# Second mixer of a two-block kernel: score, transpose and value products regrouped on TensorE, two kinds of chunks read out two pieces later

## The chip, the cores and the metric

The kernel runs on one core of a Trainium2 chip, in one launch. The metric is the device time of one execution in microseconds (us), as the median of several runs.

## What is computed

The reference runs two blocks over 256 tokens of width 2048, in float32. The first block (a short gated convolution, a conformer convolution and pooling, then a gated MLP) is untouched by the change. The second begins with one large projection, whose columns feed four mLSTM heads and eight attention heads:

```python
xn = rmsnorm(x, norm_mix_pre[l])
proj = jnp.einsum('bsd,dc->bsc', xn, w_in[l])
mq, mk, mv, mo, mi, mf, aq, ak, av, g_m, g_a = split_cols(proj)
qk = jax.nn.silu(causal_depthwise_conv_2(jnp.concatenate([mq, mk], axis=-1), conv_w[l], conv_b[l]))
...
h = mlstm_chunkwise(mq_h, mk_h, mv_h, i_pre, f_pre)
h = h * lax.rsqrt(jnp.mean(h * h, axis=-1, keepdims=True) + NORM_EPS)
...
o_a = moba_attention(aq_h, ak_h, av_h)
```

At 256 tokens an mLSTM head is a causal product of decayed scores (q times k) with the values v, normalised, gated by o. An attention head is softmax(q k) times v over one block. After that come the merge with the gates g_m and g_a, the output projection and the second MLP.

## The kernel before, in words

The program is written engine by engine, with semaphores between them, and its order is written out by hand. Every weight matrix goes through the same conveyor, in **pieces** of 128 x 1024 numbers. SP's queue brings 1 MB blocks (two pieces) into `raw` (4 slots). ScalarE (ACT) copies a piece to the high half of `w_split` (L1138, `split`), VectorE (DVE) subtracts to make the low half (L1777, `split`), and TensorE (PE) multiplies: 8 tiles of three matmuls, 24 in all, per piece (L700 to L702; L792 to L794 where the tokens are the stationary operand). There are 4 slots of `w_split`, so ACT and DVE may make piece n only once PE has used piece n - 4. In this stage PE takes a piece in some 2.7 us, and DVE makes one in 1.2 us and has the rest of the time for everything else.

In the second mixer the projection goes in 28 **chunks** of four pieces (`CHUNKS2`). Chunk c is pieces 4c to 4c + 3. Per mLSTM head h they are q, k, v, o (chunks 4h to 4h + 3), then per pair of attention heads j aq, ak, av (chunks 16 + 3j and on). The merge's 24 pieces per turn follow, numbered from 112. Chunks 0 and 1 are an exception: they are opened together, q ending with piece 7 and k of the first head with piece 10 as DVE and ACT count them (`ends_2`: `{0: 7, 1: 10}`); every other chunk c ends with piece 4c + 3.

What is done at the end of a chunk stands in `chunk_end_2(c, o)`, called by ACT and DVE behind the split of the piece that comes o after the chunk's last one. DVE at o == 4 reads the chunk out of PSUM (`take_scaled`, `scale_tokens`, which count `pair_combined` up; PE waits on this before it starts the chunk after the next, which has the same PSUM bank). For q and k follow: ACT at o == 5 and DVE at o == 6 the short convolution into `q_m` and `k_m`, ACT at o == 7 a tanh, and DVE at o == 8 the last product (L1780, `q_m<-squares,q_m`), which counts `qk_ready` up. `o_m` and `a_v` are single buffers.

The products of the heads themselves are dropped in between pieces. `inner(piece_number)` calls on PE, ahead of a piece, `mlstm(h, stage)` where `piece_number - 16 * (h + 1)` is in `M_PE`, and `attention(j, stage)` where `piece_number - (64 + 12 * (j + 1))` is in `A_PE`:

- `mlstm` stage 0: the scores (L986), behind a wait `qk_ready` >= 2h + 2, that is, for both q_m and k_m of the head; stage 1: the values (L992 to L994); stage 2: four transposes of h_tok (L1001).
- `attention` stage 0: the scores of two heads (L1014, L1015); stage 1: transposes of the probabilities (L1022); stage 2: the values (L1032, L1034).

`M_ACT`, `M_DVE`, `A_ACT` and `A_DVE` hold the same kind of numbers for ACT's and DVE's share of a head. Below, "r" is a piece's number less 16(h + 1), and all these products are plain float32, where the pieces are float32r.

The two lines that set where PE stands before a head's products are these:

```python
r = piece_number - 16 * (h + 1)
if r in M_PE:
    mlstm(h, M_PE.index(r))
```

Of the kernel before, what the change touches and what calls it, by code (L numbers as in the profile page):

```python
# [93 lines left out]
def build(nc, xT, params, consts, positions, w_in, w_out, w_up, w_down,  # L94
# [22 lines left out]
    with ctx:  # L117
# [14 lines left out]
        def put(name, shape):  # L132

            at = cursor[0]
            cursor[0] += (4 * math.prod(shape[1:]) + 31) // 32 * 32
            return place(name, shape, at=at)
# [68 lines left out]
        o_m = put("o_m", [128, 2, T])  # L205
# [15 lines left out]
        a_v = put("a_v", [128, 2, T])  # L221
# [18 lines left out]
        def P(name, k=0, n=1):  # L240
            at = PARAM[name] + k
            return par[:, at:at + n] if isinstance(at, int) else par[:, bass.ds(at, n)]
# [9 lines left out]
        def bcast(row, tiles=2):  # L252

            return row.rearrange("p (a t) -> p a t", a=1).to_broadcast([128, tiles, T])


        def sem(name):
            return ctx.enter_context(nc.semaphore(name))
# [102 lines left out]
        m_gated = sem("m_gated")  # L361
# [9 lines left out]
        a_valued = sem("a_valued")  # L371
# [35 lines left out]

        M_PE, M_ACT, M_DVE = (4, 9, 14), (8, 13, 15, 19), (7, 9, 12, 14, 18, 20)  # L410
        A_PE = (2, 9, 12)
        A_ACT, A_DVE = ((6, 12, 15), (7, 12, 15)), ((5, 7, 16), (6, 9, 16))
        ROWS_STORED, SCALE_STORED = 18, 12

        BOUNDARY_SPLITS = {N_PREF1: {3: (5,), 5: (6,), 6: (7,)}, N_PRE2: {3: (5,), 5: (6, 7)},
# [18 lines left out]
        def at_least(eng, s, value):  # L434

            if not isinstance(value, int) or value > 0:
                eng.wait_ge(s, value)
# [66 lines left out]
        def pair2(c):  # L504
            return qW2 + c - 1

        def last_of(first, c):

            return first(NARROW * c + 3 + {0: 4, 1: 1}.get(c, 0))
# [61 lines left out]
        def tiles_of(bank):  # L571
            return ps[:, bank, :].rearrange("p (a t) -> p a t", a=2)
# [124 lines left out]
        def _(pe):  # L697
# [340 lines left out]
            def inner(piece_number):  # L1038
# [9 lines left out]
                for j in range(4):  # L1048
                    r = piece_number - (64 + 12 * (j + 1))
                    if r in A_PE:  # L1050
                        attention(j, A_PE.index(r))

# [69 lines left out]
        def _(act):  # L1122
# [17 lines left out]
            def combined(q):  # L1140
                act.wait_ge(pair_combined, q.value(PAIR_CREDIT + 1))
# [304 lines left out]
            for g, n in enumerate(GROUPS1):  # L1446
# [13 lines left out]
                last = g == len(GROUPS1) - 1  # L1460
# [33 lines left out]
            def chunk_end_2(c, o):  # L1494

                kind, h = CHUNKS2[c]
                q = Step(pair2(c))
                if o == 5 and kind in ("q", "k"):
                    is_k = int(kind == "k")
                    out = (q_m, k_m)[is_k]  # L1500
                    if c > 1:
                        combined(q)
                    else:
                        act.wait_ge(opened, 2 + c + 1)
                    at_least(act, m_scored, h)
                    source = k_in if c == 1 else qk_in
                    for t in range(2):
                        k = 8 * is_k + 2 * h + t
                        nc.scalar.activation(out[:, t, :], source[:, t, 3:3 + T], ACT.Identity,
                                             scale=P("conv_w_2", 48 + k), bias=P("conv_b_2", k)  # L1510
                                             ).then_inc(qk_started, 1)
                elif o == 7 and kind in ("q", "k"):
                    is_k = int(kind == "k")
                    act.wait_ge(qk_convolved, 2 * h + is_k + 1)
                    nc.scalar.activation(squares[:, is_k, :, :], (q_m, k_m)[is_k][:, :, :], ACT.Tanh, scale=0.5
                                         ).then_inc(qk_tanh, 1)
                elif o == 5 and kind == "o":
                    combined(q)
                    nc.scalar.activation(o_m[:, :, :], o_m[:, :, :], ACT.Tanh, scale=0.5).then_inc(o_ready, 1)

# [228 lines left out]
        def _(dve):  # L1749
# [26 lines left out]
            def tt(out, a, b, op):  # L1776
                return nc.vector.tensor_tensor(out, a, b, op)  # L1777

            def stt(out, a, scalar, b, op0, op1):
                return nc.vector.scalar_tensor_tensor(out=out, in0=a, scalar=scalar, in1=b, op0=op0, op1=op1)  # L1780
# [9 lines left out]
            def summed(last):  # L1790

                dve.wait_ge(piece_used, last.value(USED_CREDIT + 1))

            def take_scaled(last, bank, out):

                summed(last)
                tt(out, tiles_of(bank), bcast(pre_scale[:, :]), ALU.mult).then_inc(pair_combined, 1)

            def scale_tokens(last, bank, out):

                summed(last)
                dve.wait_ge(pre_col_loaded, 16)
                for s in range(2):
                    ins = nc.vector.tensor_scalar(out[:, s, 0:T], ps[:, bank + s, 0:T], pre_col[:, s:s + 1], None,
                                                  ALU.mult)
                ins.then_inc(pair_combined, 1)
# [6 lines left out]
            def combined(q):  # L1813
                dve.wait_ge(pair_combined, q.value(PAIR_CREDIT + 1))
# [502 lines left out]
            def chunk_end_2(c, o):  # L2317
                kind, h = CHUNKS2[c]
                q, last, bank = Step(pair2(c)), Step(last_of(piece2, c)), 2 * ((c + 1) % 2)
                is_k = int(kind in ("k", "ak"))  # L2320
                if o == 4:
                    if kind in ("q", "k"):
                        if c > 1:
                            at_least(dve, qk_convolved, 2 * h + is_k)
                            take_scaled(last, bank, qk_in[:, :, 3:3 + T])
                    elif kind == "v":
                        at_least(dve, m_valued, h)
                        scale_tokens(last, bank, v_tok)
                    elif kind == "av":
                        at_least(dve, a_valued, 2 * h)  # L2330
                        scale_tokens(last, bank, a_v)
                    elif kind == "o":
                        at_least(dve, m_gated, h)
                        take_scaled(last, bank, o_m[:, :, :])
                    else:
                        at_least(dve, a_scored, 2 * h)
                        take_scaled(last, bank, {"aq": a_q, "ak": a_k}[kind][:, :, :])
                elif o == 6 and kind in ("q", "k"):
                    out = (q_m, k_m)[is_k]
                    for k in (2, 1, 0):  # L2340
                        for t in range(2):
                            if k == 2:
                                dve.wait_ge(qk_started, 4 * h + 2 * is_k + t + 1)
                            else:
                                dve.wait_ge(vector_step, steps.all(but=1))
                            ins = stt(out[:, t, :], (k_in if c == 1 else qk_in)[:, t, k:k + T], P("conv_w_2", 16 * k + 8 * is_k + 2 * h + t),
                                      out[:, t, :], ALU.mult, ALU.add)
                            if (k, t) == (0, 1):
                                ins.then_inc(qk_convolved, 1)
                            else:  # L2350
                                ins.then_inc(vector_step, steps.one())
                elif o == 8 and kind in ("q", "k"):
                    out = (q_m, k_m)[is_k]
                    dve.wait_ge(qk_tanh, 2 * h + is_k + 1)
                    stt(out[:, :, :], squares[:, is_k, :, :], 1.0, out[:, :, :], ALU.add, ALU.mult
                        ).then_inc(qk_ready, 1)
                elif o == 5 and kind in ("aq", "ak"):
                    a = (a_q, a_k)[is_k]
                    combined(q)
                    dve.wait_ge(table_step, 3)  # L2360
                    at_least(dve, rope_ready, 2 * h + is_k)
                    for lo_, hi_ in ((0, 64), (64, 0)):
                        for t in range(2):
                            tt(scaled[lo_:lo_ + 64, 0, t, :], a[hi_:hi_ + 64, t, :],
                               sin[hi_:hi_ + 64, :], ALU.mult).then_inc(vector_step, steps.one())
                    dve.wait_ge(vector_step, steps.all())
                    tt(a[:, :, :], a[:, :, :], bcast(cos[:, :]), ALU.mult).then_inc(vector_step, steps.one())
                    dve.wait_ge(vector_step, steps.all())
                    tt(a[:, :, :], a[:, :, :], scaled[:, 0, :, :], ALU.add).then_inc(rope_ready, 1)
# [278 lines left out]
```

## Time and profile before

| what | value |
|---|---|
| median of 3 runs | 2422.86 us (2422.09 to 2423.03) |
| the profiled execution's own time | 2421.82 us |
| its span, first to last instruction | 2420.0 us |
| PE busy | 2409.3 us (100%) |
| PE weight loads busy | 2395.4 us (99%) |
| DVE busy | 1631.7 us (67%) |
| ACT busy | 1186.5 us (49%) |
| SP's queue | 456.34 MB, 58.1% of the 16 DMA engines' span |
| HBM read | 455.15 MB, 189 GB/s over the span |
| mean granted TensorE clock | 0.999 |

The span is 1.8 us under the execution's own time, and that is 1.0 us under the median. A busy PE says only that matmuls follow one another closely: they are pipelined, each lasts 276 ns in the records, and in the steady parts one starts every 113 ns. So what counts is the distance of two starts. In a timeline row the first number is the start, the second the duration, and "xN" says how many instructions are merged; a float32 matmul counts as two passes there, a transpose as one. A window row gives the stretch, its length, the busy time and number of instructions (x) of PE, weight loads (PEld), DVE, ACT and POOL (only PE and PEld where it is asked for one line), then the granted clock as a share of 2.4 GHz, the DMA engines' busy share and GB/s.

### The profile page before, as it was taken

What the parts mean: (1) busy time and instruction counts of PE and PEld (TensorE: products, weight loads), DVE (VectorE), ACT (ScalarE), POOL (GpSimd) and SP (SyncE); (2) the same over time, 40 slices, a digit from 0 to 9 for tenths busy, and PEclk for the clock granted to TensorE, in tenths of its full rate; (3) what the DMA queues carried; (4) which work ended last, traced back from release to release, by engine and by line L of the source; (5) the groups of instructions that cost most, each with busy time, mean ns of one, the idle gap of its engine ahead of it and who ended that gap; (6) DMA issues with size and microseconds to landing.
All of it is one profiled execution on the core that took longest, in us unless ns stands there. A gap on an engine that the chain in (4) does not pass through costs nothing. (4 is left out here: it accounts for less than half of the span.)

```text
span 2420.0 us, 49137 instructions
## 1 busy us (share of the span) xinstructions
PE 2409.3 (100%) x20938; PEld 2395.4 (99%) x20938; DVE 1631.7 (67%) x2088; ACT 1186.5 (49%) x1434; POOL 58.9 (2%) x57
## 2 busy tenths in 40 slices
PE   9999999999999999999999999999999999999999
PEld 9999999999999999999999999999999999999998
DVE  8998687765776567697677655554865554555554
ACT  6445655534554455666544444445543443443444
POOL 0300100000000000100000000001000000000001
PEclk9999999999999999999999999999999999999999
DMA  8565555565555555565555566655555655655652
GB/s 286 185 192 192 175 197 196 182 208 192 191 191 194 194 195 192 167 206 175 178 179 171 185 187 196 194 193 192 171 195 194 193 198 194 196 192 191 192 193 104
DMA packets 308084, 459.64 MB, mean 190 GB/s; under 512 B 14789, under 2 KB 156370, under 8 KB 307922
## 3 DMA queue, kind: packets, MB, share of 16 engines
q1 hardware_dynamic: 304112, 456.34, 58.1%
q8 instruction: 126, 2.06, 0.3%
q10 hardware_dynamic: 3810, 0.94, 0.2%
q14 instruction: 36, 0.29, 0.0%
HBM read 455.15 MB, written 2.11 MB: 189 GB/s over the span
## 5 line engine op out<-in xcount | busy, mean ns | idle before, releaser
L1777 DVE TENSOR_TENSOR w_split<-raw,w_split 128x1024 fp32r<-128x1024 f32 (+1 forms) x856 | 1047.2, 1225 | 747.3 <-ACT w_split L1138 744.8
L1138 ACT ACTIVATE w_split<-raw 128x1024 fp32r<-128x1024 f32 x853 | 900.6, 1060 | 1064.6 <-PE ps L702 1020.3
L700 PE MATMUL ps<-h_split,w_split 128*128 128x256 f32 x3904 | 1081.6, 277 | 0.3 <-DVE w_split L1777 0.3
L701 PE MATMUL ps<-h_split,w_split 128*128 128x256 f32 x3904 | 1078.4, 276 | 0.0
L702 PE MATMUL ps<-h_split,w_split 128*128 128x256 f32 x3904 | 1078.3, 276 | 0.0
L700 PEld LDWEIGHTS ps<-h_split,w_split 128*128 128x128 f32 x3904 | 732.9, 188 | 0.9 <-DVE w_split L1777 0.5
L701 PEld LDWEIGHTS ps<-h_split,w_split 128*128 128x128 f32 x3904 | 732.9, 188 | 0.3
L702 PEld LDWEIGHTS ps<-h_split,w_split 128*128 128x128 f32 x3904 | 732.8, 188 | 0.0
L700 PE MATMUL ps<-act_split,w_split 128*128 128x256 f32 x2240 | 619.3, 276 | 0.0
L701 PE MATMUL ps<-act_split,w_split 128*128 128x256 f32 x2240 | 618.3, 276 | 0.0
L702 PE MATMUL ps<-act_split,w_split 128*128 128x256 f32 x2240 | 618.3, 276 | 0.0
L701 PEld LDWEIGHTS ps<-act_split,w_split 128*128 128x128 f32 x2240 | 420.4, 188 | 0.1
L700 PEld LDWEIGHTS ps<-act_split,w_split 128*128 128x128 f32 x2240 | 420.4, 188 | 0.1
L702 PEld LDWEIGHTS ps<-act_split,w_split 128*128 128x128 f32 x2240 | 420.4, 188 | 0.0
L1780 DVE SCALAR_TENSOR_TENSOR conv_b<-glu,par,conv_b 128x256 f32<-128x256 f32 x180 | 80.4, 501 | 0.0
L792 PE MATMUL ps<-w_split,h_split 128*128 128x256 f32 x256 | 72.2, 282 | 0.0
L793 PE MATMUL ps<-w_split,h_split 128*128 128x256 f32 x256 | 71.0, 277 | 0.0
L794 PE MATMUL ps<-w_split,h_split 128*128 128x256 f32 x256 | 71.0, 277 | 0.0
L700 PE MATMUL ps<-merged,w_split 128*128 128x256 f32 x256 | 70.9, 277 | 0.0
L702 PE MATMUL ps<-merged,w_split 128*128 128x256 f32 x256 | 70.7, 276 | 0.0
L701 PE MATMUL ps<-merged,w_split 128*128 128x256 f32 x256 | 70.7, 276 | 0.0
L1725 POOL TENSOR_TENSOR square_sum<-squares 128x512 f32<-128x512 f32 x4 | 6.6, 1647 | 2081.9 <-ACT squares L1151 2081.9
(290 smaller groups left out, 1613.3 us busy)
## 6 DMA issues: line engine op xcount, KB each, us to landing
raw<-w_up SPq DMA_DIRECT2D x152, 1024.0 KB, 5.1
raw<-w_in SPq DMA_DIRECT2D x114, 1024.0 KB, 5.3
raw<-w_down SPq DMA_DIRECT2D x108, 1024.0 KB, 5.0
raw<-w_out SPq DMA_DIRECT2D x32, 1024.0 KB, 5.0
raw<-w_in SPq DMA_DIRECT2D x16, 512.0 KB, 5.2
raw<-w_branch_m SPq DMA_DIRECT2D x8, 1024.0 KB, 5.3
raw<-w_branch_a SPq DMA_DIRECT2D x8, 1024.0 KB, 5.3
outT<-x SPq DMA_DIRECT2D x7, 256.0 KB, 2.3
```

The source lines that it names most:

```text
L700: nc.tensor.matmul(out, hi[:, cols], rhs[:, k, 0:T], start=start, stop=False)
L701: nc.tensor.matmul(out, hi[:, cols], rhs[:, k, T:2 * T], start=False, stop=False)
L702: return nc.tensor.matmul(out, lo[:, cols], rhs[:, k, 0:T], start=False, stop=stop)
L792: nc.tensor.matmul(out, high, pair[:, 0, cols], start=k == 0, stop=False)
L793: nc.tensor.matmul(out, high, pair[:, 1, cols], start=False, stop=False)
L794: last = nc.tensor.matmul(out, rest, pair[:, 0, cols], start=False, stop=k == 15)
L1138: nc.scalar.activation(split_home(n)[0], raw[:, slot, half:half + 1024], ACT.Copy).then_inc(hi_ready, 1)
L1725: nc.gpsimd.tensor_tensor(square_sum[:, :, :], square_sum[:, :, :] if q > 1 else squares[:, 0, :, :], squares[:, q % 2, :, :], ALU.add).th ...
L1777: return nc.vector.tensor_tensor(out, a, b, op)
L1780: return nc.vector.scalar_tensor_tensor(out=out, in0=a, scalar=scalar, in1=b, op0=op0, op1=op1)
```

## The change

Two tables of numbers and two readouts are different:

- `M_PE` goes from (4, 9, 14) to (0, 9, 16). Head h's scores now stand ahead of piece 16(h + 1), four pieces earlier. Its transposes stand ahead of piece 16(h + 2), two pieces later, in front of the next head's scores. Its share on DVE and ACT behind the transposes is one piece later (18 to 19, 20 to 21; 19 to 20).
- `A_PE` goes from (2, 9, 12) to (2, 9, 14). A pair's values now stand in front of the next pair's scores, and what DVE and ACT do with them is two pieces later (16 to 18; 15 to 17).
- The o chunks and the av chunks are read out at o == 6, not at o == 4, and ACT's tanh of o comes at o == 7, not at o == 5.

```diff
-        M_PE, M_ACT, M_DVE = (4, 9, 14), (8, 13, 15, 19), (7, 9, 12, 14, 18, 20)
-        A_PE = (2, 9, 12)
-        A_ACT, A_DVE = ((6, 12, 15), (7, 12, 15)), ((5, 7, 16), (6, 9, 16))
+        M_PE, M_ACT, M_DVE = (0, 9, 16), (8, 13, 15, 20), (7, 9, 12, 14, 19, 21)
+        A_PE = (2, 9, 14)
+        A_ACT, A_DVE = ((6, 12, 17), (7, 12, 17)), ((5, 7, 18), (6, 9, 18))
...
-                elif o == 5 and kind == "o":
+                elif o == 7 and kind == "o":
                     combined(q)
                     nc.scalar.activation(o_m[:, :, :], o_m[:, :, :], ACT.Tanh, scale=0.5).then_inc(o_ready, 1)
...
-                    elif kind == "av":
-                        at_least(dve, a_valued, 2 * h)
-                        scale_tokens(last, bank, a_v)
-                    elif kind == "o":
-                        at_least(dve, m_gated, h)
-                        take_scaled(last, bank, o_m[:, :, :])
-                    else:
+                    elif kind in ("aq", "ak"):
                         at_least(dve, a_scored, 2 * h)
                         take_scaled(last, bank, {"aq": a_q, "ak": a_k}[kind][:, :, :])
+                elif o == 6 and kind == "av":
+                    at_least(dve, a_valued, 2 * h)
+                    scale_tokens(last, bank, a_v)
+                elif o == 6 and kind == "o":
+                    at_least(dve, m_gated, h)
+                    take_scaled(last, bank, o_m[:, :, :])
```

**TensorE, the first head's scores.** `w_split0` to `w_split3` are the four slots; the rows before are the end of piece 15 (slot 1), the start of piece 16 (slot 2), and, four pieces on, the end of piece 19 (slot 1 again) with the scores behind it.

```order
6472 L702 MATMUL ps<-h_split_55,w_split1_51 128x256
6473 L700 MATMUL ps<-h_split_55,w_split2_52 128x256 [waits lo_ready,pair_combined]
...
6568 L702 MATMUL ps<-h_split_55,w_split1_51 128x256
6569 L986 MATMUL ps<-q_m_88,k_m_89 128x256 [waits qk_ready,pair_combined]
6570 L986 MATMUL ps<-q_m_88,k_m_89 128x256
6571 L986 MATMUL ps<-q_m_88,k_m_89 128x128 x2
```

The same place in the changed kernel:

```order
6472 L702 MATMUL ps<-h_split_55,w_split1_51 128x256
6473 L986 MATMUL ps<-q_m_88,k_m_89 128x256 [waits qk_ready,pair_combined]
6474 L986 MATMUL ps<-q_m_88,k_m_89 128x256
6475 L986 MATMUL ps<-q_m_88,k_m_89 128x128 x2
6476 L700 MATMUL ps<-h_split_55,w_split2_52 128x256 [waits lo_ready]
```

The first head's scores, with their wait for `qk_ready`, have moved from behind piece 19 to right behind piece 15, with no transposes in front of them, since there is no head before.

**VectorE, the same stretch.** These rows run from the split of piece 16 to that of piece 21, in the kernel before; the changed one has the same rows as far as number 870.

```order
859 L1777 TENSOR_TENSOR w_split2_52<-raw_49,w_split2_52 128x1024 [waits hi_ready]
860 L1780 SCALAR_TENSOR_TENSOR k_m_89<-k_in_106,par_57,k_m_89 128x256 [waits qk_started] x2
861 L1780 SCALAR_TENSOR_TENSOR k_m_89<-k_in_106,par_57,k_m_89 128x256 [waits vector_step] x4
862 L1777 TENSOR_TENSOR w_split3_53<-raw_49,w_split3_53 128x1024 [waits hi_ready]
...
868 L1777 TENSOR_TENSOR w_split0_50<-raw_49,w_split0_50 128x1024 [waits hi_ready]
869 L1780 SCALAR_TENSOR_TENSOR k_m_89<-squares_61,k_m_89 128x512 [waits qk_tanh]
870 L1777 TENSOR_TENSOR w_split1_51<-raw_49,w_split1_51 128x1024 [waits hi_ready]
871 L1777 TENSOR_TENSOR o_m_90<-ps,pre_scale_66 128x512 [waits piece_used]
872 L1777 TENSOR_TENSOR w_split2_52<-raw_49,w_split2_52 128x1024 [waits hi_ready]
873 L1777 TENSOR_TENSOR w_split3_53<-raw_49,w_split3_53 128x1024 [waits hi_ready]
```

The last product of the first head's k_m (869) stands behind the split of piece 18 (868), before and after the change; what moved is the readout of o_m, from 871 to behind 873.

**TensorE, transposes and the next head's scores** in the changed kernel, ahead of piece 32, the first pair of this kind; the transposes stood alone ahead of piece 30, the scores alone ahead of piece 36.

```order
6863 L1001 MATMUL ps<-con_58,h_tok_94 128x128 [waits h_tok_ready,pair_combined]
6864 L1001 MATMUL ps<-con_58,h_tok_94 128x128 x3
6865 L986 MATMUL ps<-q_m_88,k_m_89 128x256 [waits qk_ready]
6866 L986 MATMUL ps<-q_m_88,k_m_89 128x256
6867 L986 MATMUL ps<-q_m_88,k_m_89 128x128 x2
6868 L700 MATMUL ps<-h_split_55,w_split2_52 128x256 [waits lo_ready]
```

Of the 23 places between pieces at which the heads' products interrupted the projection 18 are left: three pairs of heads' transposes and scores and three of values and scores now share a place, and the last mLSTM head's transposes, which shared one with the first attention pair's scores (ahead of piece 78), stand alone ahead of piece 80.

## Rows read from the trace of the kernel before

**Rows 1.** The page, busy time of the engines.

```profile
PE 2409.3 (100%) x20938; PEld 2395.4 (99%) x20938; DVE 1631.7 (67%) x2088; ACT 1186.5 (49%) x1434; POOL 58.9 (2%) x57
```

**Rows 2.** Window over the second mixer: busy time of PE, PEld, DVE, ACT, POOL.

```profile
1041.00:1401.00 360.00, 360.00 (x3079) 357.73 (x3078) 265.22 (x429) 189.54 (x260) 0.00 (x0) 1.00 0.59 181
```

**Rows 3.** Waits of PE in the whole span: in total, times, longest.

```profile
PE ps L700 <- DVE w_split L1777: 0.3, 1, 0.3
```

**Rows 4.** Timeline of PE: transposes alone, scores alone, both together.

```profile
1105.62 0.28 PE L702 MATMUL ps<-h_split,w_split 128*128 128x256 f32 x1
...
1106.29 0.28 PE L701 MATMUL ps<-h_split,w_split 128*128 128x256 f32 x1
...
1283.64 0.28 PE L702 MATMUL ps<-h_split,w_split 128*128 128x256 f32 x1
...
1285.18 0.28 PE L701 MATMUL ps<-h_split,w_split 128*128 128x256 f32 x1
...
1246.91 0.28 PE L702 MATMUL ps<-h_split,w_split 128*128 128x256 f32 x1
1247.03 0.60 PE L1001 MATMUL ps<-con,h_tok 128*128 128x128 f32 x4
...
1248.89 0.28 PE L701 MATMUL ps<-h_split,w_split 128*128 128x256 f32 x1
```

**Rows 5.** Timeline of PE, and line L700 in a window: pieces 12 to 19.

```profile
1053.24 0.28 PE L794 MATMUL ps<-w_split,h_split 128*128 128x256 f32 x1
...
1053.36:1064.44 11.08, 8.90 (x32) 5.99 (x33) 1.00 0.62 189
...
1064.44 0.28 PE L700 MATMUL ps<-h_split,w_split 128*128 128x256 f32 x1
...
1069.98 0.38 PE L700 MATMUL ps<-h_split,w_split 128*128 128x256 f32 x1
...
1075.55 1.47 PE L986 MATMUL ps<-q_m,k_m 128*128 128x256 f32 x8
```

**Rows 6.** Timeline of DVE, first head: k_m's convolution to its last product.

```profile
1062.55 2.46 DVE L1780 SCALAR_TENSOR_TENSOR k_m<-k_in,par,k_m 128x256 f32<-128x256 f32 x6
1064.93 1.22 DVE L1777 TENSOR_TENSOR w_split<-raw,w_split 128x1024 fp32r<-128x1024 f32 x1
...
1068.72 1.21 DVE L1777 TENSOR_TENSOR w_split<-raw,w_split 128x1024 fp32r<-128x1024 f32 x1
1069.86 0.67 DVE L1780 SCALAR_TENSOR_TENSOR k_m<-squares,k_m 128x512 f32<-128x512 f32 x1
```

**Rows 7.** Timeline of PE at the span's start and end; a window behind it.

```profile
1.78 1.49 PE L892 MATMUL ps<-val_b 128*128 128x256 f32 x3
...
2.63 1.80 PE L892 MATMUL ps<-val_b 128*128 128x256 f32 x4
...
4.70 1.24 PE L892 MATMUL ps<-val_b 128*128 128x256 f32 x5
8.03 0.38 PE L736 MATMUL ps<-h_split,w_split 128*128 128x256 f32 x1 [2.09 <-DVE w_split L1777]
...
2410.91 4.46 PE L1117 MATMUL ps<-y,con 128*128 128x512 f32 x10
...
2416.00:2418.00 2.00, 0.00 (x0) 0.00 (x0) 0.00 (x0) 0.00 (x0) 0.00 (x0) 0.85 1.05 406
```

**Rows 8.** Timeline of PE: start of piece 32, end of piece 35.

```profile
1111.83 0.28 PE L700 MATMUL ps<-h_split,w_split 128*128 128x256 f32 x1
...
1122.60 0.28 PE L702 MATMUL ps<-h_split,w_split 128*128 128x256 f32 x1
```

**Rows 9.** Timeline of DVE, second head: k_m, o_m, piece 37's split.

```profile
1103.46 0.68 DVE L1780 SCALAR_TENSOR_TENSOR k_m<-squares,k_m 128x512 f32<-128x512 f32 x1
...
1114.27 0.68 DVE L1777 TENSOR_TENSOR o_m<-ps,pre_scale 128x512 f32<-128x512 f32 x1
...
1118.57 1.23 DVE L1777 TENSOR_TENSOR w_split<-raw,w_split 128x1024 fp32r<-128x1024 f32 x1 [0.64 <-ACT w_split L1138]
```

## Prediction

> **What bounds the kernel now.** I began with the page's busy times, because they say which engine to follow: TensorE is busy for all of the span, and so in the second mixer too, 360 of 360 us, while DVE has 265 us and ACT 190 us of work there [rows 1, 2]. Then I read PE's waits. Over the whole span only 0.3 us of waiting is put down to an ordinary piece at L700, once, and none to a score, a transpose or a value product [rows 3]. So this stage lasts as long as PE's stream of matmuls. A change of order can win only what an interruption of that stream costs beyond its own matmuls, and it can lose by putting a wait where PE stands with nothing else to do. The timelines of PE and DVE price both.
>
> **What joining is worth.** From piece 32 to the end of piece 35 nothing interrupts: 95 distances between 1111.83 and 1122.60, or 0.1134 us each, 2.72 us a piece [rows 8]. Now the interruptions, each measured from the last piece matmul ahead of it to the second one behind it, less two such ordinary distances (0.23 us) [rows 4]:
> - transposes alone: 1106.29 - 1105.62 - 0.23 = 0.44 us
> - scores alone (attention's): 1285.18 - 1283.64 - 0.23 = 1.31 us
> - transposes and scores together, which the kernel has once: 1248.89 - 1246.91 - 0.23 = 1.75 us
>
> 0.44 + 1.31 is 1.75. Joined they cost what they cost apart, so the restart that one would expect to save is not there. The change makes six joins and undoes one; I put them at 5 x 0.00 = 0. No join of values and scores is in the trace. From below a join could cost 0.02 us (rounding of the rows); from above it can save no more than the piece matmul's slower restart, some 0.1 us, so 0 to 0.6 us for six. I take 0, being nearest to the one join that is there. One more thing could be won: behind the transposes the matmuls of pieces 30 and 31 start 0.118 us apart (1106.29 to 1111.83, 47 distances) against 0.1134 [rows 4, 8]. I count some 20 such pieces in the stage, 0.11 us each, 2.2 us in all. They are not all behind an interruption, so I take 0 and keep 1 us for the range.
>
> **The later readouts.** PE needs a bank back before the chunk after the next. For the second head that is piece 36, whose predecessor's last matmul starts at 1122.60 [rows 8]. The o readout now follows the split of piece 37, which DVE ends at 1118.57 + 1.23 = 1119.80 at present; with 0.68 us more it is over at 1120.5 [rows 9]. Margin 2.1 us, and both sides move together when PE's products move. Cost 0. The readout waits for the head before to be gated, and the gate product now stands two places ahead of it on DVE, whose input (transposes ahead of piece 32) is made before DVE reaches it. ACT's tanh of o and the later shares of a head move by one or two pieces with nobody on PE waiting closely. No DMA is issued differently. Cost 0.
>
> **The scores, four pieces earlier.** For the second head k_m is finished at 1103.46 + 0.68 = 1104.1, and PE now asks for it ahead of piece 32, at 1111.8: 7.7 us to spare [rows 8, 9]. The first head is another matter. The token chunk of pieces 8 to 11 ends with L794 at 1053.24; L700 has then 32 matmuls, 8 to a piece, up to 1064.44; so that is the start of piece 16 [rows 5]. It is there that the changed PE stands before the scores and waits for `qk_ready` >= 2. In DVE's queue k_m's last product comes behind a convolution of 2.46 us, a split, the small gate rows and another split, and it ends at 1069.86 + 0.67 = 1070.53 [rows 6]. In the kernel before, the scores came at 1075.55 [rows 5], 5 us after that; this is what the four pieces in between were hiding. Nothing in the change makes DVE or ACT quicker ahead of this product, and nothing that they do up to it needs a piece behind piece 14, so PE's pause does not delay them either. The working:
> - hand-over from DVE to PE: a split ends at 1068.72 + 1.21 = 1069.93 and piece 18's first matmul is at 1069.98, 0.05 us [rows 5, 6]
> - new pause: 1070.53 + 0.05 - 1064.44 = **6.14 us**
> - what it takes away: pieces 16 to 19 now last 1075.55 - 1064.44 = 11.11 us where 96 x 0.1134 = 10.89 us would do; the 0.2 us is piece 18's wait for its split [rows 5], which is ready long before once PE has paused: -0.2 us
> - sum: **+5.9 us**
>
> PE has no later idle time in which this could be made up [rows 2, 3]. What is queued behind the waiting scores is the whole projection.
>
> **The clock.** A pause of 6 us may cost more than itself. The last matmuls, ten passes from 2410.91, end at 2415.37; the window from 2416 to 2418 has a mean clock of 0.85, so the clock fell from 1.0 (2.4 GHz) to 0.5 (1.2 GHz) at about 2417.4, 2.0 us behind the last matmul [rows 7]. Against that, a pause of 2.09 us ahead of 8.03 did no harm that the rows show [rows 7]. Ours is three times as long, so I expect it to fall. What it costs then I take from the start: the first passes at L892 are 0.425 us apart (two between 1.78 and 2.63), those from 4.70 on (1.24 - 0.38) / 4 = 0.215 us. With the first at about 1.2 and the change at about 4.2 that is 3.0 us at half speed, and half of it, **1.5 us**, is lost. Bounds: 0, if the clock stays, and 3 us, if it needs twice as long. The Trainium skill ("TensorE: Matmul & The Clock Gate", section on HAM oscillation) says that a stall in a stream of matmuls throws the clock back and tells of 1.67 us throttled for each such stall; as an estimate from that page, half of it, 0.8 us, would be lost, and the time would be 2429.6 us. The startup row is this chip's own and gives the larger loss; no pause of this length is in the trace.
>
> **Sum.** 0 for the joins, 0 for the readouts, +5.9 for the pause, +1.5 for the clock: +7.4 us. Against the profiled execution's 2421.82 us that is 2429.2 us; this execution is 1.0 us below the median of the runs, 2422.86 us, so the predicted median is 2422.86 + 7.4 = **2430.3 us**, +0.31%. What a measurement of this kernel can tell from no change is about 0.2%, 4.8 us.
>
> **Rivals.**
> 1. *The pause without the clock.* The clock's fall depends on how the pause lies; then +5.9 us, 2428.8 us. For: the pause of 2.09 us went by unpunished. Against: the fall 2.0 us behind the last matmul. Still slower by 0.24%. Chance 0.2.
> 2. *Not slower: the stream gets smoother by more than a microsecond.* The place is the 20 pieces whose matmuls are 0.118 us apart. If what slows them is the restart behind scattered products, and the joins and the pause (which lets DVE catch up) remove most of them, 2 us come back: 5.9 - 2.0 = +3.9 us without a fallen clock, 2426.8 us, within 0.2%. It decides from 1.1 us of gain on. Against it: some of these pieces stand ahead of an interruption. Chance 0.07.
> 3. *No pause, because PE gets to the first scores later than I read or DVE's product comes earlier.* The change would then do nothing but the joins: 2422.9 us. The order of both engines speaks against it: the scores stand directly behind piece 15, and DVE's rows ahead of the product are the same as before. Chance 0.03.
> 4. *Faster*: as 3, with the slow pieces gone and some restarts saved, 2.2 + 0.6 us at most, 2420.1 us. That is not 0.2% even so; it would take a source that I don't see. Chance 0.02.
>
> **The numbers.** My forecast, pause and fallen clock, has 0.68. Slower by over 0.2% are the forecast and rival 1, 0.88, and a little of rival 2: 0.89. Within 0.2%: the rest of rival 2 and rival 3, 0.09. Faster 0.02. The range has to hold rival 1 less the microsecond kept for smoother pieces, 2427.8 us, and at the top a clock that stays low twice as long, 2431.8 us, with half the spread of the runs (0.5 us) and some hand-over time on it: 2432.6 us.
>
> **What would show it.** In PE's waits of the changed kernel a single new row, L986 for DVE's k_m (L1780), of some 6 us, at about 1064.4; no such row for the other three heads. In a window just behind it a clock under 1.0, and matmuls at distances of 0.21 us for about 3 us. PE's wait at piece 18 gone. Transposes with the next scores at the same 1.75 us as apart. The forecast is wrong if the pause is missing or under 5 us, if the clock stays at 1.0 (then rival 1), or if PE waits for a readout of o or av.

## The result and the profile after

| | before | after |
|---|---|---|
| median of 6 runs each | 2422.64 us (2422.09 to 2423.69) | 2431.58 us (2431.23 to 2432.17) |
| the profiled execution's own time | 2421.82 us | 2431.39 us |
| its span | 2420.0 us | 2429.6 us |
| mean granted clock | 0.999 | 0.998 |

The changed kernel is slower: ratio 1.0038, 95% interval 1.0028 to 1.0048, 8.9 us by the medians. The forecast was 2430.3 us with a range of 2427.8 to 2432.6; it was right in sign and range and 1.3 us short.

PE's waits over the whole span, in the changed kernel (engine, line, what it waited for; then us in total, times, the longest one), answer to [rows 3]:

```profile
PE ps L986 <- DVE k_m L1780: 6.4, 1, 6.4
...
PE ps L700 <- DVE w_split L1777: 0.3, 1, 0.3
```

One row is new, and it occurs once: of four heads only the first waits for its k_m. The window of the second mixer, beside [rows 2], has PE at 353.65 us of 360, and a clock under 1:

```profile
1041.00:1401.00 360.00, 353.65 (x2993) 351.23 (x2992) 259.63 (x424) 186.22 (x256) 0.00 (x0) 0.99 0.58 177
```

The timeline of PE at the first head's scores (start, duration, engine, line, operation):

```profile
1063.90 0.28 PE L702 MATMUL ps<-h_split,w_split 128*128 128x256 f32 x1
1070.53 2.90 PE L986 MATMUL ps<-q_m,k_m 128*128 128x256 f32 x8 [6.35 <-DVE k_m L1780]
1073.08 0.56 PE L700 MATMUL ps<-h_split,w_split 128*128 128x256 f32 x1
1073.44 0.41 PE L701 MATMUL ps<-h_split,w_split 128*128 128x256 f32 x1
...
1076.21 0.33 PE L702 MATMUL ps<-h_split,w_split 128*128 128x256 f32 x1
1076.38 0.28 PE L700 MATMUL ps<-h_split,w_split 128*128 128x256 f32 x1
```

And DVE's, which ends the wait:

```profile
1068.57 1.21 DVE L1777 TENSOR_TENSOR w_split<-raw,w_split 128x1024 fp32r<-128x1024 f32 x1
1069.71 0.67 DVE L1780 SCALAR_TENSOR_TENSOR k_m<-squares,k_m 128x512 f32<-128x512 f32 x1
```

k_m is over at 1069.71 + 0.67 = 1070.38, 0.15 us before it stood in the kernel before [rows 6], and PE goes on at 1070.53. Without a wait PE would have gone on at 1063.90 + 0.11 = 1064.01, so the pause is 6.52 us. Behind it the scores last 2.90 us, where they lasted 1.47 [rows 5], and 14 distances from 1073.44 to 1076.38 make 2.94 us, 0.21 us each: half speed. From 1076.38 on the distance is 0.12 us again.

The granted clock is the third number from the end of a window row:

```profile
1066.00:1068.00 2.00, 0.00 (x0) 0.00 (x0) 1.90 (x5) 0.48 (x1) 0.00 (x0) 1.00 0.37 70
1068.00:1070.00 2.00, 0.00 (x0) 0.00 (x0) 1.97 (x4) 1.00 (x1) 0.00 (x0) 0.87 1.07 380
1070.00:1072.00 2.00, 1.47 (x4) 1.23 (x5) 1.52 (x2) 0.06 (x1) 0.00 (x0) 0.50 0.27 89
...
1076.00:1078.00 2.00, 2.00 (x17) 2.00 (x17) 0.00 (x0) 0.30 (x1) 0.00 (x0) 0.92 1.21 270
```

0.87 is a clock at 1.0 (2.4 GHz) for 1.5 us and at 0.5 (1.2 GHz) for 0.5 us, so it fell at about 1069.5, in the pause; 0.92 puts its return at about 1076.3. PE worked 5.8 us at half speed.

**Where the time went.** I numbered the pieces in both traces (the first values, L992, stand ahead of piece 25, and a piece is 24 matmuls) and took the lag, that is the start of a piece in this kernel less its start in the kernel before:

| stretch of pieces | lag, us | change |
|---|---|---|
| 9, before anything is changed | -0.53 | chance; -0.95 to 1.39 in the profiled executions below |
| 15 to 21 (pause, low clock) | -0.43 to 8.82 | +9.25 |
| 21 to 83 (the mLSTM joins) | 8.82 to 8.34 | -0.48 |
| 87 to 117 (the attention joins) | 8.35 to 9.55 | +1.20 |
| 117 to 138, end of the stage | 9.55 to 9.54 | 0 |

That is 10.0 us in the stage, against 9.6 us between the spans and 8.9 us between the medians; a single pair of executions is good to about 1 us, for the reason in the first line. From piece 21 on the lags repeat to 0.1 us in all kernels below that have the same order at a place, and I argue from them. Ahead of it they don't: from piece 15 to 21 one and the same order gives +1.47, +1.56 and +2.17 us in e1_first4, e4_mlstm_joins and e9_dummy12, so +9.25 is good to about half a microsecond.

### The profile page after: what moved, and what is told of

Same layout as the page of the kernel before. It is cut to its first block, busy times and chain, and to the rows that moved or that the text cites. A ratio compares the mean times of both kernels' runs of the same rounds, so it can differ in the third digit from the quotient of the medians.

```text
span 2429.6 us, 49137 instructions
## 1 busy us (share of the span) xinstructions
PE 2413.2 (99%) x20938; PEld 2399.1 (99%) x20938; DVE 1631.0 (67%) x2088; ACT 1186.6 (49%) x1434; POOL 58.9 (2%) x57
## 4 chain that ended last, share of the span: by engine, by line
PE 55%; DVE 1%; issue 1%; ACT 0%; DMA 0%; ACTq 0%; DVEq 0%
PE ps L700 17%; PE ps L702 17%; PE ps L701 16%; PE ps L793 1%; PE ps L792 1%; PE ps L794 1%; DVE w_split L1777 0%; PE ps L736 0%; PE ps L740 0%; PE ps L737 0%; PE ps L986 0%; DVE square_sum L1777 0%; PE ps L1117 0%; PE ps L818 0%; PE ps L1015 0%
## 5 line engine op out<-in xcount | busy, mean ns | idle before, releaser
L700 PE MATMUL ps<-h_split,w_split 128*128 128x256 f32 x3904 | 1082.2, 277 | 0.3 <-DVE w_split L1777 0.3
L700 PEld LDWEIGHTS ps<-h_split,w_split 128*128 128x128 f32 x3904 | 733.8, 188 | 0.7 <-DVE w_split L1777 0.4
L700 PE MATMUL ps<-act_split,w_split 128*128 128x256 f32 x2240 | 619.3, 276 | 0.0
L700 PEld LDWEIGHTS ps<-act_split,w_split 128*128 128x128 f32 x2240 | 420.5, 188 | 0.1
L700 PE MATMUL ps<-merged,w_split 128*128 128x256 f32 x256 | 70.9, 277 | 0.0
```

What stands on the lines that cost most here:

```text
L700: nc.tensor.matmul(out, hi[:, cols], rhs[:, k, 0:T], start=start, stop=False)
```

## The experiments

Each ran in 5 rounds beside the kernel before, whose median was 2422.5 us in the first two groups and 2422.19 us for the last kernel. In the table "pause" is PE's wait for k_m and "clock" the lowest granted clock in a 2 us window behind it.

| kernel | median, us | ratio, 95% | pause, us | clock |
|---|---|---|---|---|
| e2_first0_alone | 2430.62 | 1.0033 [1.0021, 1.0045] | 6.6 | 0.50 |
| e3_filled | 2428.91 | 1.0026 [1.0016, 1.0035] | 0.6 | 1.00 |
| e5_first1 | 2428.53 | 1.0025 [1.0015, 1.0035] | 3.5 | 0.52 |
| e6_first2 | 2423.74 | 1.0006 [0.9997, 1.0016] | 0.9 | 1.00 |
| e1_first4 | 2423.56 | 1.0004 [0.9995, 1.0013] | 0 | 1.00 |
| e7_attn_joins | 2423.69 | 1.0005 [0.9996, 1.0014] | 0 | 1.00 |
| e4_mlstm_joins | 2422.66 | 1.0001 [0.9992, 1.0010] | 0 | 1.00 |
| e9_dummy12 | 2424.26 | 1.0008 [0.9999, 1.0017] | 0 | 1.00 |
| e10_first_o4 | 2422.26 | 1.0000 [0.9991, 1.0009] | 0 | 1.00 |

**The first head back to its old place** (e1_first4). The changed kernel, with the first head's scores ahead of piece 20 again:

```diff
-                    if r in M_PE:
-                        mlstm(h, M_PE.index(r))
+                    at = M_PE if h else (4, *M_PE[1:])
+                    if r in at:
+                        mlstm(h, at.index(r))
```

> The changed kernel with the first head's scores alone back ahead of piece 20; everything else of the change stays. Theory A (the pause for the first head's k_m, and the clock that falls in it, are all of the loss): PE's wait at L986 is gone, the granted clock stays at 1.0 up to the end, and the time is 2422.6 plus what the joins cost in the trace of the changed kernel behind piece 21 (its lag on the kernel before goes from 8.8 to 9.5 us, so +0.7): 2423.3 us, between 2422.3 and 2424.0. Theory B (the later readouts and the crowded stretches on DVE cost a good part): 2425 us or more, with waits of PE behind piece 30.

Measured: 2423.56 us (2423.20 to 2424.18), within theory A's range; 8.0 us of the changed kernel's excess are gone, with the pause and the low clock. So nearly all of it came from one place, the scores of one head. About 1 us stays by the medians, which the interval can't tell from nothing. The trace shows a wait that neither kernel had. On PE:

```profile
1077.09 1.57 PE L986 MATMUL ps<-q_m,k_m 128*128 128x256 f32 x8 [0.70 <-DVE o_m L1778]
```

and on DVE:

```profile
1076.35 0.68 DVE L1778 TENSOR_TENSOR o_m<-ps,pre_scale 128x512 f32<-128x512 f32 x1
```

The scores ahead of piece 20 also carry piece 20's wait for its bank (`pair_combined`), and the bank comes free only when the first head's o chunk is read out, at 1076.35 + 0.68 = 1077.03. This is the readout that the change puts behind two more splits. In the changed kernel the scores are done by then, and the bank is first needed by piece 20 itself, 1.23 us later in the order.

**The first head's move alone** (e2_first0_alone). The kernel before, and nothing changed but this:

```diff
-                    if r in M_PE:
-                        mlstm(h, M_PE.index(r))
+                    at = M_PE if h else (0, *M_PE[1:])
+                    if r in at:
+                        mlstm(h, at.index(r))
```

> The kernel before with one thing of the change alone: the first head's scores ahead of piece 16. Theory A: one wait of PE at L986 of some 6.3 us, the clock down to 0.5 some 5.5 us behind PE's last matmul, and +8.5 to +9.4 us, 2431.1 to 2432.0 us. Theory B: clearly less than that, 2429 us or below, since the joins and the readouts are not in it.

Measured: 2430.62 us, 8.1 us above the kernel before and 0.5 us under the least that theory A gave. The lag is 8.45 us from piece 21 to the end of the stage: no gain or loss elsewhere. PE and then the clock:

```profile
1071.01 2.90 PE L986 MATMUL ps<-q_m,k_m 128*128 128x256 f32 x8 [6.60 <-DVE k_m L1781]
```

```profile
1066.00:1068.00 2.00, 0.00 (x0) 0.00 (x0) 1.90 (x4) 0.97 (x2) 0.00 (x0) 1.00 0.21 26
1068.00:1070.00 2.00, 0.00 (x0) 0.00 (x0) 1.96 (x3) 0.51 (x1) 0.00 (x0) 0.52 1.00 329
...
1074.00:1076.00 2.00, 2.00 (x15) 2.00 (x15) 0.00 (x0) 0.00 (x0) 0.00 (x0) 0.78 0.93 254
```

The pause is 0.25 us longer than in the changed kernel, but the clock fell at about 1068.1 and was back at about 1074.9. It was low for 6.8 us in both; here 3.9 us of that fell on work, so some 1.9 us were lost by half of it, where the changed kernel lost 2.7 (measured below). In these two traces the price of nearly the same pause differs by some 0.8 us with the moment at which the clock falls in it. Theory A had taken that moment from the changed kernel's trace, hence its half microsecond too much.

**The pause filled with work** (e3_filled). The changed kernel, with 14 float32 matmuls ahead of the first head's wait. They add work whose result is overwritten, and leave nothing out:

```diff
+                    if h == 0:
+                        for i in range(FILLERS):
+                            nc.tensor.matmul(ps[:, 4, 0:T], ones, K("identity", 0, T), start=True, stop=True)
                     pe.wait_ge(qk_ready, 2 * h + 2)
```

> The changed kernel with 14 float32 matmuls of 256 columns on constants ahead of the wait (about 14 x 0.43 = 6.0 us on PE, results overwritten by the scores). PE stands before the first scores as long as before, but is not idle. Theory A with the clock as its second term: the clock stays at 1.0 and 5.6 us of PE work at half speed are run at full speed, so 2.8 us less than the changed kernel, 2428.8 us (2428.3 to 2429.5). Rival C (the clock's fall costs nothing of its own, the pause is longer than I think): 2431.6 us as the changed kernel.

Measured: 2428.91 us (2427.99 to 2429.55), 2.7 us less than the changed kernel with more work in it. The same wait is there, but PE is busy in it:

```profile
1064.29 6.20 PE L985 MATMUL ps<-con 128*128 128x256 f32 x28
1071.14 1.57 PE L990 MATMUL ps<-q_m,k_m 128*128 128x256 f32 x8 [0.65 <-DVE k_m L1784]
1072.47 0.36 PE L701 MATMUL ps<-h_split,w_split 128*128 128x256 f32 x1
...
1074.28 0.28 PE L701 MATMUL ps<-h_split,w_split 128*128 128x256 f32 x1
```

```profile
1070.00:1074.00 4.00, 3.35 (x24) 2.85 (x23) 2.22 (x3) 0.77 (x1) 0.00 (x0) 1.00 0.56 160
```

From the scores' start to the 16th piece matmul behind them it is 74.28 - 71.14 = 3.14 us here and 76.38 - 70.53 = 5.85 us in the changed kernel: 2.71 us. The clock's share is shown twice, by the medians and by the rows.

**Fewer pieces earlier** (e5_first1, e6_first2). The edit of e1_first4 with 1 and with 2 in place of 4.

> The changed kernel with the first head's scores ahead of piece 17, one piece later than in the change. PE gets there 2.7 us later and waits for the same product of DVE, some 3.8 us instead of 6.4. Theory A: in three runs so far the clock fell 4 to 5.6 us behind PE's last matmul, so here it may or may not fall; if it stays, 2423.6 (the version with the scores ahead of piece 20) + 3.8 - 0.5 = 2426.9 us; if it falls shortly before the pause ends, up to 2.8 us more, 2429.7 us. The granted clock of the windows decides which. Rival F (what is lost does not follow the length of the pause): 2431.6 us as for the change.

> The changed kernel with the first head's scores ahead of piece 18. PE gets there some 1 us before DVE has the product. Theory A: a wait of about 1.1 us at L986, no fall of the clock, and since PE waited 0.5 to 1.2 us for splits in this stretch anyway, 2423.6 + 0 to 1.1 us: 2423.6 to 2424.7 us. Rival F: 2427 us or more.

Measured: 2428.53 us (2427.79 to 2429.29) and 2423.74 us (2423.29 to 2424.94). PE at the scores in the one and in the other:

```profile
1072.18 2.93 PE L986 MATMUL ps<-q_m,k_m 128*128 128x256 f32 x8 [3.47 <-DVE k_m L1781]
```

```profile
1070.58 1.57 PE L986 MATMUL ps<-q_m,k_m 128*128 128x256 f32 x8 [0.95 <-DVE k_m L1781]
```

The pause shrinks by 2.9 and 2.5 us with the first and the second piece in front of the scores, about a piece's 2.7 to 2.8 us each: 6.35, 3.47, 0.95. The clock doesn't go by such even steps. With one piece in front:

```profile
1070.00:1072.00 2.00, 0.00 (x0) 0.00 (x0) 2.00 (x3) 1.06 (x1) 0.00 (x0) 1.00 1.08 380
1072.00:1074.00 2.00, 1.82 (x4) 1.51 (x5) 1.26 (x2) 0.32 (x1) 0.00 (x0) 0.52 0.08 25
1074.00:1076.00 2.00, 2.00 (x12) 1.96 (x11) 1.23 (x1) 0.74 (x1) 0.00 (x0) 0.63 0.81 250
```

It fell at about 1072.1, when the scores were about to start at 1072.18, and was back at about 1075.5; nearly all of the 3.4 us fell on work and 1.65 us were lost. So in this execution, the slowest of the nine, a pause of 3.5 us costs 5.2 us (lag 1.38 at piece 15, 6.57 at piece 21). The median is 6.0 us above the kernel before; less the 0.7 us of the joins' part, -0.5 and +1.2, that is 5.3 us. It lies between theory A's two cases, the clock staying (2426.9 us) and falling for all of 2.8 us (2429.7 us). From place 0 to 1 the medians give back 3.1 us, from 1 to 2 another 4.8.

**The joins by halves** (e4_mlstm_joins, e7_attn_joins). The first has the mLSTM part of the change with the first head's scores at their old place, the second only the attention part. Against the changed kernel, e4_mlstm_joins has this (with the av chunk read out at o == 4 again and the edit of e1_first4):

```diff
-        A_PE = (2, 9, 14)
-        A_ACT, A_DVE = ((6, 12, 17), (7, 12, 17)), ((5, 7, 18), (6, 9, 18))
+        A_PE = (2, 9, 12)
+        A_ACT, A_DVE = ((6, 12, 15), (7, 12, 15)), ((5, 7, 16), (6, 9, 16))
```

And e7_attn_joins this (with the o chunk read out at o == 4 and its tanh at o == 5 again):

```diff
-        M_PE, M_ACT, M_DVE = (0, 9, 16), (8, 13, 15, 20), (7, 9, 12, 14, 19, 21)
+        M_PE, M_ACT, M_DVE = (4, 9, 14), (8, 13, 15, 19), (7, 9, 12, 14, 18, 20)
```

> Only the mLSTM part of the change (transposes ahead of the next head's scores, o read out two pieces later), with the first head's scores ahead of piece 20, attention as in the kernel before. In the changed kernel's trace the lag goes from 8.8 to 8.3 us over these heads. Theory D (the joins win nothing in the interruption itself, but fewer pieces run at the slower matmul distance): 0.5 us less than the kernel before, 2422.1 us. Rival E (joins change nothing): 2422.6 us. Either is within 0.5 us of the other, so the distances of pieces in the trace have to decide.

> Only the attention part of the change (a pair's values ahead of the next pair's scores, av read out two pieces later), mLSTM as before. In the trace of the changed kernel the lag on the kernel before grows by 0.4 us at each of the three joined pairs, because pieces 88 to 91 and their like run at 2.83 us and not 2.72. Theory D: the same here, so +1.2 us, 2423.7 us, and a joined interruption of 2.62 us as apart. Rival E (this comes from the mLSTM part's shift against the attention): 2422.5 us.

Measured: 2422.66 us (2422.20 to 2424.02) and 2423.69 us (2422.88 to 2424.58). The medians alone can't tell either from the kernel before; the lags can. In the mLSTM half the lag goes from 0.73 at piece 21 to 0.24 at piece 70 and stays; in the attention half it is 0.53 to 0.54 from piece 18 to 87, then 0.94, 1.33 and 1.74 behind the three pairs. That is -0.5 and +1.2 us, as in the changed kernel.

It isn't the joins themselves. The transposes with the next scores in the changed kernel:

```profile
1119.88 0.28 PE L702 MATMUL ps<-h_split,w_split 128*128 128x256 f32 x1
1119.99 0.60 PE L1001 MATMUL ps<-con,h_tok 128*128 128x128 f32 x4
1120.43 1.47 PE L986 MATMUL ps<-q_m,k_m 128*128 128x256 f32 x8
1121.66 0.37 PE L700 MATMUL ps<-h_split,w_split 128*128 128x256 f32 x1
1121.86 0.28 PE L701 MATMUL ps<-h_split,w_split 128*128 128x256 f32 x1
```

1121.86 - 1119.88 - 0.23 = 1.75 us, what the two cost apart. A pair's values alone in the kernel before:

```profile
1276.88 0.28 PE L794 MATMUL ps<-w_split,h_split 128*128 128x256 f32 x1
...
1278.42 0.28 PE L701 MATMUL ps<-h_split,w_split 128*128 128x256 f32 x1
```

1.54 - 0.23 = 1.31 us. Joined with the scores in e7_attn_joins, with the pieces around them:

```profile
1277.53 0.28 PE L700 MATMUL ps<-h_split,w_split 128*128 128x256 f32 x1
...
1280.35 0.28 PE L700 MATMUL ps<-h_split,w_split 128*128 128x256 f32 x1
...
1283.06 0.28 PE L702 MATMUL ps<-h_split,w_split 128*128 128x256 f32 x1
1283.18 0.59 PE L1032 MATMUL ps<-prob_t,a_v 128*128 128x256 f32 x2
...
1285.92 0.28 PE L701 MATMUL ps<-h_split,w_split 128*128 128x256 f32 x1
...
1288.63 0.28 PE L700 MATMUL ps<-h_split,w_split 128*128 128x256 f32 x1
...
1291.46 0.28 PE L700 MATMUL ps<-h_split,w_split 128*128 128x256 f32 x1
...
1294.18 0.28 PE L700 MATMUL ps<-h_split,w_split 128*128 128x256 f32 x1
```

2.86 us, less 0.24 us at this place's distance, is 2.62 us, and 1.31 + 1.31 is 2.62. A join is worth nothing. What changed is the pace of whole pieces: 1277.53 to 1280.35 (piece 88) is 2.82 us and 1288.63 to 1291.46 (piece 91) 2.83 us, or 0.118 us a matmul; the next, piece 92, is 2.72 us, 0.1133. Four pieces a pair, 88 to 91, 100 to 103 and 112 to 115, go at the slow pace with the attention joins and at the fast one without: 4 x 0.1 us = 0.4 us a pair. In the mLSTM half it goes the other way: pieces 30 and 31 were slow behind lone transposes [rows 4], so were 62, 63, 78 and 79, and these six are fast now, while 80 and 81 have become slow; four fewer are -0.4 to -0.5 us. In the changed kernel pieces 30 and 31 start here:

```profile
1114.55 0.28 PE L700 MATMUL ps<-h_split,w_split 128*128 128x256 f32 x1
...
1117.27 0.28 PE L700 MATMUL ps<-h_split,w_split 128*128 128x256 f32 x1
```

From piece 28 on, the kernels with the same order at a place have the same slow pieces there.

**Does a short interruption bring back the fast pace?** (e9_dummy12) In the kernel before, a pair's values stand ahead of piece 88, which is where the slow pace begins without them. One float32 matmul with an unused result goes there, and at the same place of the other three pairs, in e1_first4 (added work, nothing left out):

```diff
+                    if r == 12:
+                        nc.tensor.matmul(ps[:, 7, 0:128], ones, identity, start=True, stop=True)
                     if r in A_PE:
                         attention(j, A_PE.index(r))
```

> The version with the first head's scores ahead of piece 20 and all joins, and one float32 matmul of 128 columns on constants (its result is overwritten) where the attention's values stood before the change, ahead of pieces 88, 100, 112 and 124. Theory G (the first float32 product behind a token chunk ends the stretch of slower pieces that follows it): pieces 88 to 91 go back to 2.72 us but for the restarts, 0.4 us less per pair for 0.3 us of interruption, so about the same total, 2423.3 to 2423.6 us, but with another pattern of pieces. Rival H (slow pieces come from the join itself): 88 to 91 stay at 2.83 us and the time is 4 x 0.3 = 1.2 us more, 2424.8 us.

Measured: 2424.26 us (2423.84 to 2426.46), 0.7 us above e1_first4, with intervals that overlap. It lies between theory G (at most 2423.6 us) and rival H (2424.8 us), so the pieces have to say. PE in piece 88 (its second matmul and the first of piece 89), and in piece 91 (its first and that of piece 92):

```profile
1280.44 0.28 PE L701 MATMUL ps<-h_split,w_split 128*128 128x256 f32 x1
...
1283.06 0.28 PE L700 MATMUL ps<-h_split,w_split 128*128 128x256 f32 x1
...
1291.23 0.28 PE L700 MATMUL ps<-h_split,w_split 128*128 128x256 f32 x1
...
1294.06 0.28 PE L700 MATMUL ps<-h_split,w_split 128*128 128x256 f32 x1
```

23 distances in 2.62 us are 0.114 us each: pieces 88 and 89 are fast. 24 in 2.83 us are 0.118: behind the joined values and scores, pieces 90 and 91 are slow, as they were. So half of the pattern followed the interruption, and neither theory holds as it was put. It wins nothing: the matmul with its restart costs 0.2 us, which is what two fast pieces give back, and the lag grows by 0.43 us a pair, where it grew by 0.40 in e1_first4. Why the scores alone leave a fast pace behind them and the values with the scores a slow one stays open.

**The readout of the first head** (e10_first_o4). e4_mlstm_joins, with the first head's o chunk read out behind the split of piece 19 again:

```diff
+                    elif kind == "o" and h == 0:
+                        take_scaled(last, bank, o_m[:, :, :])
                     elif kind in ("aq", "ak"):
...
-                elif o == 6 and kind == "o":
+                elif o == 6 and kind == "o" and h:
```

> The four mLSTM joins as in e4_mlstm_joins, attention as in the kernel before, and only the first head's o chunk read out at o == 4 again instead of o == 6. Theory R (the later readout of the first head is a cost of its own, which the pause of the changed kernel hides): PE's wait of 0.5 us at L986 for DVE's o_m ahead of piece 20 disappears, the span is 0.5 us shorter than that of e4_mlstm_joins, the lag behind the kernel before is 0.2 us at piece 20 and about -0.3 us from piece 70 to the end, and the median is some 2422.2 us, 0.3 us below the kernel before, which a measurement can't tell from it. Rival S (the wait is there because PE comes to that place sooner and would move to the next readout or split): PE waits 0.5 us elsewhere between pieces 20 and 24, the span is that of e4_mlstm_joins, and the median stays at 2422.7 us.

Measured: 2422.26 us (2421.01 to 2423.88), with the kernel before at 2422.19. At piece 18 PE waits for its split in both kernels; from there to piece 20 the lag goes from -0.10 to -0.11 us here and from -0.21 to 0.73 in e4_mlstm_joins. In e4_mlstm_joins DVE ended the readout at 1075.44 + 0.68 = 1076.12 and PE went on at 1076.17, after 0.49 us. In this kernel, first PE, then DVE:

```profile
1075.45 1.47 PE L986 MATMUL ps<-q_m,k_m 128*128 128x256 f32 x8
```

```profile
1071.49 0.67 DVE L1778 TENSOR_TENSOR o_m<-ps,pre_scale 128x512 f32<-128x512 f32 x1
```

The wait is gone, and it had cost 0.9 us, more than its own 0.5. The profile counts a wait from the end of the matmul before; from start to start it is 0.64 us. The scores behind a wait last 0.1 us longer (1.57 against 1.47 us), and pieces 18 and 19 were slow ones there, 0.2 us together. Theory R holds for the wait and its place; the span is 1.0 us shorter than that of e4_mlstm_joins, where it had expected 0.5. The medians show neither: e4_mlstm_joins is 0.14 us above the kernel before and e10_first_o4 0.07 us, each against its own rounds. From piece 18 to the end of the stage its lag goes from -0.10 to -0.58 us, the half microsecond of the mLSTM part; that too is a statement about the trace, not a gain that the medians show.

## Why the prediction was right, and where its steps were off

- **The pause** was forecast at 6.14 us, at this place, for this product, for this head alone. It is 6.52. PE came 0.43 us sooner to it (1064.01 for 1064.44), DVE 0.15 us sooner, and the hand-over took 0.15 us, not 0.05: 0.43 - 0.15 + 0.10 = 0.38. Rival 3 (no pause) is out by the row L986 <- k_m.
- **PE's wait at piece 18** is gone, as said.
- **The clock** was the mis-sized term: 1.5 us forecast, 2.7 measured (e3_filled, twice). I took 3 us at half speed from the kernel's start; behind this pause PE worked 5.8 us at half speed. The bound of 3 us for the loss held, the value didn't. The start was a single draw, as the same fourteen passes at L892 show, in the kernel before and in e1_first4:

```profile
1.19 4.75 PE L892 MATMUL ps<-val_b 128*128 128x256 f32 x14 [1.19 <-DVE val_b L1921]
```

```profile
1.19 6.15 PE L892 MATMUL ps<-val_b 128*128 128x256 f32 x14 [1.19 <-DVE val_b L1922]
```

In e1_first4 all of them are at half speed, 0.43 us apart. Over the eleven profiled executions the clock rose between 2.9 us (e3_filled) and 5.9 us (e5_first1) behind the first matmul, so the same reading of another execution would have given up to twice the 1.5 us. I had also placed the fall about 2 us behind the last matmul's end, from the end of the kernel [rows 7], which is 2.6 us behind its start; it came 5.6 us behind the last start here and 3.9 in e2_first0_alone. The Trainium skill ("TensorE: Matmul & The Clock Gate", section on HAM oscillation) says that a stall throws the clock back, and the traces agree for the pauses of 6.6, 6.35 and 3.5 us, not for those of 0.9 and 2.09 us. Its 1.67 us throttled for a stall is from another kernel and is no price for this pause, where the clock was low for 6.8 us. Rival 1, the pause alone at 2428.8 us, is close to e3_filled's 2428.91 us, but in part by luck: the 0.7 us of pieces' pace is in that too.
- **The sum** was +7.4 against +8.9 by the medians; 1.2 of the 1.5 missing are the clock, 0.4 the pause. By the lags there are +0.7 us of pieces' pace besides (below). These terms together make 9.7 us, 0.8 more than the medians show and 0.3 less than the lags, which is as far as a single pair of traces goes; that the forecast came within 1.3 us owes something to this.
- **The joins at 0** were right in themselves: 1.75 and 2.62 us are the sums of the parts. But the step "they are not all behind an interruption, so I take 0" left out that an order decides which pieces are slow: -0.5 us for the mLSTM part and +1.2 for attention. Rival 2 (a smoother stream, 2 us back) was right for six pieces and wrong for fourteen.
- **The later readouts at 0** held in the changed kernel, but I had worked out the margin for the second head alone and carried it over to the first, where DVE is late with k_m. With the first head's scores ahead of piece 20 PE waits 0.5 to 1.0 us there (e1_first4, e4_mlstm_joins, e9_dummy12), which costs 0.9 to 1.2 us, and e10_first_o4 takes it away in the trace. I had put its absence from the changed kernel down to the long pause. The traces say that the place of the scores is enough: with them ahead of piece 18, behind a pause of only 0.9 us, DVE has read o_m out at 1075.64 + 0.69 = 1076.33 and PE comes to piece 20 at 1077.45 with no wait (e6_first2).

```profile
1075.64 0.69 DVE L1778 TENSOR_TENSOR o_m<-ps,pre_scale 128x512 f32<-128x512 f32 x1
```

Not tried: moving k_m's last product ahead of a split on DVE, which would shorten the pause without moving the scores.

## What to carry to other kernels

When an operation is moved earlier for every round of a loop, work out the first round by itself: its producer has had no time to run ahead, and one head of four made all of the loss. A pause of the busy engine is priced with its clock: by the lags of one execution each, 6.5 us cost 9.2, and 3.5 us cost 5.2, while one of 0.9 us cost only itself; by the medians less the 0.7 us of pieces' pace it is 8.2, 5.3 and 0.6 us. A figure for the clock that is read from one execution is one draw; read the same place in several. And a readout that costs nothing in one order may cost something once the operation that first needs its bank is moved: look again before calling it free.

## What the runs showed of the hardware

- The clock fell 5.6 us behind the last matmul's start in the changed kernel's pause, 3.9 us in that of e2_first0_alone and 3.65 us in that of e5_first1, and at the kernels' ends between 2.6 us (the kernel before) and 5.6 us (e3_filled); it did not fall in pauses of 0.9 and 2.09 us. Once it had fallen inside a long pause it stayed low for 6.8 us in both kernels, for 3.4 us in e5_first1. Matmuls of no use in the pause kept it at 1.0 and saved 2.7 us.
- The steady distance of these matmuls has two levels, 0.1133 and 0.118 us, at a granted clock of 1.0, for whole pieces at a time. From piece 28 on, which pieces are slow repeats for one order and changes with the order; those that changed did so two at a time. What decides it I couldn't find.
